# 192 turns (128x128 transposes) move from TensorE to VectorE's 32x32 blocks and a scratch in DRAM

## The chip, the cores and the metric

One core of one Trainium2 chip runs one program. The metric is the device time of that program in microseconds (us), the median of several runs. TensorE is called PE, VectorE DVE, ScalarE ACT, GpSimd POOL and SyncE SP, as the profile does.

## The reference, cut to what matters

```python
# x: (1, 256, 2048) float32; one layer
h = rmsnorm(x, g_mix)
q_r, f_r, i_r, og_r, q_a, k_a, v_a, gate_a, gate_b = split_columns(h @ w_in)
# (A) gated linear recurrence, 16 heads of 128, chunks of 64 positions
f = lb + (1 - lb) * sigmoid(f_r); k = 1 - f; b = cumsum(log f) in a chunk
a = (silu(q_r) * exp(b - b_mid)) @ (k * exp(b_mid - b)).T, causal
o_a = a @ i_r + (q * exp(b)) @ state, normed, * silu(og_r)
# (B) attention over a band of 2 chunks, 32 heads of 64, 4 key heads, rotary, a sink
pr = softmax([q k^T, sink]); o_b = pr @ v
x = x + concat(sigmoid(gate_a) * o_a, sigmoid(gate_b) * o_b) @ w_out
h = rmsnorm(x, g_mlp)
x = x + square(relu(h @ w_up)) @ w_down
x = x + sigmoid(x @ w_ple_gate) * (p @ w_ple_proj)
return rmsnorm(x, g_final)
```

## The kernel before, in words

All weights stream from DRAM once, in 588 chunks of 256 rows x 512 columns (512 KB). A chunk is loaded by SP into one of `RAW_SLOTS` = 4 buffers (`w_raw`). ACT then copies it to a rounded float (`w_hi`, line 977, in `split_hi`) and DVE subtracts to get the rest (`w_lo`, line 1334, in `split_lo`), each into one of `W_SLOTS` = 4 buffers. PE multiplies: per chunk four matmuls of the activations' high part and four of their low part with `w_hi` (lines 678 and 679), then four with `w_lo` (line 684). The buffers come back in order: SP's load of chunk n waits for `w_lo` of chunk n-4, ACT's split of chunk n waits until PE has used chunk n-4.

The work between the products is written into the same order by hand. Each engine has a function `steps(n)`. PE calls it behind chunk n; ACT and DVE run `LAG` = 3 chunks ahead of it, so they call `steps(n)` behind their split of chunk n+3. All waits are in the order of the program on each engine: whoever waits holds up everything behind it there, the splits of later chunks too.

Before the output projection of the mixer there are four head groups (j = 0 to 3), each with blocks of 8 chunks: qa, gb, f, q, then i, og, ga (for j > 0 the 16 chunks of the output projection of the group before, `wo`, stand between q and i). A position in group j is counted from the first chunk of f: `a = n - A0[j]` for the attention, `h = n - H0[j]` for the recurrence; both have the same zero. The tables `SCORES`, `F_TURN`, `Q_TURN`, `DECAY`, `KE_TURN` and others say at which position a step stands.

PE turns what the products leave with positions on partitions into channels on partitions, by a product with an identity matrix (`turn`, line 720, and `weights_turn`, line 759) into a PSUM bank: per group the rotated queries (`zb`, 8 turns), f (`za`, 8), q (`zb`, 8), the attention weights (`pr`, 16) and the merge gate (`sgb`, 8). ACT or DVE takes each from PSUM (for `pr`: DVE's copy to `pT`, line 1490). The turns of `x_sb`, `u_sb`, and `gate` are others, and stay. `weighted_values` is the product of the turned weights with the values (line 771), `scores` the product of line 747, and `recurrence_scores` and `late_scores` (lines 787, 791, 804) use what DVE makes of f and q; PE waits there for `ke_ready` (line 1641).

After the mixer come the 128 `up` chunks, of which the last 112 have the weights as the stationary operand (`turned_chunk`, lines 692 and 698), the `down` chunks, and the gate at the end.

Of the kernel before, what the change touches and what calls it, by code (L numbers as in the profile page):

```python
# [34 lines left out]
P = 128  # L35
TT = 2
# [97 lines left out]
def program(nc, x, p, positions, g_mix, w_in, lb_logits, hgrn_norm_g, sinks, w_out,  # L134
            g_mlp, w_up, w_down, w_ple_gate, w_ple_proj, g_final, out):
    with ExitStack() as ctx:
# [29 lines left out]
        with ExitStack() as mix:  # L166
# [25 lines left out]
            pT = mb("pT", [P, 2, 4, P])  # L192
# [79 lines left out]
        kTd_out = sem("kTd_out")  # L272
        qaT_out = sem("qaT_out")
        nm_ready = sem("nm_ready")
        pr_ready = sem("pr_ready")
        pT_out = sem("pT_out")
# [50 lines left out]
        out_stored = sem("out_stored")  # L327

# [94 lines left out]
        for j in range(NG):  # L423
            for t in range(TT):
                use(("qaT", j, t), t, qaT_out, 2 * j + t + 1)
            for t in range(TT):
                for hh in range(2):
                    use(("score", j, t, hh), hh, pr_ready, 4 * (2 * j + t + 1))
                for g in range(2):
                    use(("pT", j, t, g), g, pT_out, 2 * (2 * j + t) + g + 1)  # L430
            use(("pv", j, 1), 0, pv_out, 2 * j + 2)
            for t in range(TT):
                use(("gbT", j, t), t, am_ready, 2 * j + t + 1)
            for hp in range(2):
                use(("fT", j, hp), 2, f_exp, 2 * j + hp + 1)
                if hp == 0:
                    use(("pv", j, 0), 2, pv_out, 2 * j + 1)
                use(("qT", j, hp), 3, q_ready, 2 * j + hp + 1)
                use(("late", j, hp), 2, late_out, 2 * j + hp + 1)
                use(("aT", j, hp), 3, am_masked, 2 * j + hp + 1)  # L440
# [81 lines left out]
        def parts_of(t):  # L522

            return ((slice(0, CHUNK), CHUNK), (slice(CHUNK, P), P)) if t == 0 else ((slice(0, P), P),)

# [7 lines left out]
        def _(sp):  # L533
# [40 lines left out]

            for slot in HEAD:
                load(slot)
                if slot[0] in (1, 2, 3):
                    load_x(slot[0])
            for r in range(ROUNDS):
                for slot in BODY:  # L580
                    load(slot, r)
# [60 lines left out]
        def _(pe):  # L642
# [9 lines left out]
            def chunk(slot, r=0):  # L652
# [13 lines left out]

                s = n % W_SLOTS
                pe.wait_ge(w_hi_ready, count(n + 1, r, LOOP_CHUNKS))
                if turned(kind, j):
                    turned_chunk(n, col, c, s, first, last, r)  # L670
                    return
# [16 lines left out]
            def turned_chunk(n, col, c, s, first, last, r):  # L688

                for kk in range(2):  # L690
                    for ct in range(4):
                        pe.matmul(turned_acc(col, ct)[:], w_hi[:, s, kk, ct * P:(ct + 1) * P],  # L692
                                  hT[:, 2 * c + kk].rearrange("p a t c -> p (a t c)"),
                                  start=first and kk == 0, stop=False)
                pe.wait_ge(w_lo_ready, count(n + 1, r, LOOP_CHUNKS))
                for kk in range(2):
                    for ct in range(4):
                        mm = pe.matmul(turned_acc(col, ct)[:, 0:TT * P], w_lo[:, s, kk, ct * P:(ct + 1) * P],  # L698
                                       hT_hi[:, 2 * c + kk].rearrange("p t c -> p (t c)"), start=False,
                                       stop=last and kk == 1)  # L700
                mm.then_inc(w_used, 1)
# [24 lines left out]
            def head_turn(kind, j, hp, src):  # L726

                turn((kind, j, hp), lambda i: src[:, i % 2, (2 * hp + i // 2) * P:(2 * hp + i // 2 + 1) * P])

# [22 lines left out]
            def weights_turn(j, t, g):  # L752
                name = ("pT", j, t, g)
                pe.wait_ge(pn_ready, 2 * (2 * j + t) + g + 1)
                signal, value = bank_free(name)
                pe.wait_ge(signal, value)
                for i in range(4):
                    hh, pair = i // 2, 2 * g + i % 2
                    mm = pe.transpose(bank(name)[:, i * P:(i + 1) * P], pr[:, pair, hh, 0:P], ident[:])  # L759
                mm.then_inc(full(name), 1)  # L760

            def weighted_values(j, t):

                name = ("pv", j, t)
                pe.wait_ge(pT_out, 2 * (2 * j + t + 1))
                signal, value = bank_free(name)
                pe.wait_ge(signal, value)
                parts_ = ((0, slice(0, P)),) if t == 0 else ((V_MIXED, slice(0, CHUNK)), (V_LATE, slice(CHUNK, P)))
                for v, qs in parts_:
                    for hh in range(2):  # L770
                        mm = pe.matmul(four(bank(name)[hh * HD:(hh + 1) * HD, :])[:, :, qs], vv[:, v, j, :],  # L771
                                       pT[:, hh, :, qs], start=True, stop=True, skip_group_check=True)
# [58 lines left out]
            def steps(n):  # L831
# [4 lines left out]
                for j in range(NG):  # L836
                    a, h = n - A0[j], n - H0[j]
                    if a == -3:
                        for t in range(TT):
                            pe.wait_ge(qa_rotated, 2 * j + t + 1)  # L840
                            turn(("qaT", j, t), lambda i: zb[:, t, i * P:(i + 1) * P])
                    for t in range(TT):
                        if a == SCORES[t]:
                            scores(j, t)
                            if t == 1:
                                weighted_values(j, 0)
                        for g in range(2):
                            if a == SCORES[t] + 7 + 2 * g:
                                weights_turn(j, t, g)
                    if a == PV1:  # L850
                        weighted_values(j, 1)
                    if a == ATT_END:
                        for t in range(TT):
# [97 lines left out]
        def _(act):  # L951
# [27 lines left out]

            def sum_squares(t, stage, squares):  # L980
# [32 lines left out]
            def exponentials(j, t, pair):  # L1013

                if pair == 0:
# [5 lines left out]
                    if j or t:  # L1021
                        act.wait_ge(pT_out, 2 * (2 * j + t))
# [11 lines left out]
            def steps(n):  # L1034
# [29 lines left out]
                for j in range(NG):  # L1064
# [3 lines left out]
                    if a == -2:  # L1068
                        for t in range(TT):
                            act.wait_ge(full(("qaT", j, t)), nth(("qaT", j, t)))  # L1070
                            act.activation(qT[:, :, t, :], four(bank(("qaT", j, t))[:]), ACT.Copy)\
# [19 lines left out]
                    if a == ATT_END + 1:  # L1091
                        for t in range(TT):
                            act.wait_ge(am_ready, 2 * j + t + 1)
                            act.activation(mT_hi[:, 4:8, t, :], four(sgb[:, t]), ACT.Copy).then_inc(moA_hi, 1)
# [7 lines left out]
                    if h == OG_END[j]:  # L1102

                        if j:
                            act.wait_ge(gated, 2 * j)
                        z_out("og", j, eg, og_exp, ACT.Exp, NR)
                    if h == GA_END[j]:
                        act.wait_ge(qa_rotated, 2 * (j + 1))
                        if j:
                            act.wait_ge(gated, 2 * j)  # L1110
                        z_out("ga", j, eg2, ga_exp, ACT.Exp, NR)
# [13 lines left out]
                    for hp in range(2):  # L1125
                        i = 2 * j + hp
                        if h == F_TURN[hp] + 1:
                            act.wait_ge(full(("fT", j, hp)), nth(("fT", j, hp)))
# [687 lines left out]
```

## Time and profile before

| | |
|---|---|
| median of 3 runs | 1716.59 us (1716.02 to 1717.23) |
| the profiled execution, its own time | 1718.0 us |
| its span, first to last instruction | 1716.3 us |
| PE busy | 1696.1 us, 99% |
| DVE busy | 1102.8 us, 64% |
| ACT busy | 925.0 us, 54% |
| DMA moved | 315.30 MB, mean 184 GB/s |

The table says what share of the span an engine had an instruction under way. Waits are in other views: a row that ends with an arrow names what the engine waited for, and the rows of a timeline give start and duration of each instruction, so that the step from one start to the next is what an instruction costs a busy engine.

### The profile page before, as it was taken

The numbers are of one execution on the slowest core, as the hardware profiler recorded it, in microseconds if no ns is written. First come the engines' busy times: TensorE is split into PE (matmuls) and PEld (weight loads), VectorE is DVE, ScalarE is ACT, GpSimd is POOL, SyncE is SP. The second block draws the span as 40 slices with busy tenths as digits, with TensorE's granted clock in tenths as the row PEclk, the third lists the DMA queues.
The fourth block names the chain that finished last, engine by engine and source line by source line (L and its number), as shares of the span: only waits on it lengthen the run. The fifth ranks groups of instructions, "written<-read, shape, count | busy, mean of one in ns | idle before, by whom it ended". The sixth has DMA issues, their size and how long they took to land.

```text
span 1716.3 us, 22351 instructions
## 1 busy us (share of the span) xinstructions
PE 1696.1 (99%) x8669; PEld 1416.6 (83%) x8669; DVE 1102.8 (64%) x1405; ACT 925.0 (54%) x1227; POOL 16.9 (1%) x72
## 2 busy tenths in 40 slices
PE   7999999999999999999999999999999999999997
PEld 6888888788887888878888888888888888888886
DVE  6667866875668756687585565656555556566565
ACT  6466647655565555655546554544444445454454
POOL 3000000000000000000000000000000000000000
PEclk9999999999999999999999999999999999999999
DMA  6655555556655566555556666666666665655554
GB/s 216 203 174 180 173 173 168 176 176 181 185 180 173 173 183 185 173 173 176 181 177 212 186 192 191 190 190 193 190 193 188 194 189 193 190 190 187 181 184 136
DMA packets 163292, 315.30 MB, mean 184 GB/s; under 512 B 10161, under 2 KB 10482, under 8 KB 163058
## 3 DMA queue, kind: packets, MB, share of 16 engines
q1 hardware_dynamic: 162016, 312.01, 59.5%
q10 hardware_dynamic: 1170, 1.87, 0.3%
q8 instruction: 68, 1.11, 0.3%
q14 instruction: 38, 0.31, 0.1%
HBM read 311.74 MB, written 2.10 MB: 183 GB/s over the span
## 4 chain that ended last, share of the span: by engine, by line
PE 98%; DVE 1%; ACT 1%; DMA 0%; issue 0%; SPq 0%; DVEq 0%; ACTq 0%
PE acc L678 22%; PE acc L679 22%; PE acc L684 22%; PE acc L692 6%; PE turn L692 6%; PE turn L678 3%; PE turn L679 3%; PE turn L684 3%; PE turn L698 3%; PE acc L698 3%; PE turn L720 2%; PE turn L747 0%; PE turn L771 0%; PE turn L820 0%; PE turn L759 0%; DMA w_raw<-in_w_in_dram 0%
## 5 line engine op out<-in xcount | busy, mean ns | idle before, releaser
L1334 DVE TENSOR_TENSOR w_lo<-w_raw,w_hi 128x1024 fp32r<-128x1024 f32 x588 | 720.0, 1224 | 562.9 <-ACT w_hi L977 560.2
L977 ACT ACTIVATE w_hi<-w_raw 128x1024 fp32r<-128x1024 f32 x588 | 622.7, 1059 | 700.7 <-PE acc L684 444.9
L678 PE MATMUL acc<-w_hi,hT 128*128 128x512 f32 x1104 | 435.6, 395 | 4.4 <-ACT w_hi L977 4.4
L679 PE MATMUL acc<-w_hi,hT 128*128 128x512 f32 x1104 | 431.1, 390 | 0.0
L684 PE MATMUL acc<-w_lo,hT 128*128 128x512 f32 x1104 | 296.2, 390 | 0.0
L678 PEld LDWEIGHTS acc<-w_hi,hT 128*128 128x128 f32 x1104 | 207.8, 188 | 48.4 <-ACT w_hi L977 5.6
L684 PEld LDWEIGHTS acc<-w_lo,hT 128*128 128x128 f32 x1104 | 207.8, 188 | 43.6
L679 PEld LDWEIGHTS acc<-w_hi,hT 128*128 128x128 f32 x1104 | 208.0, 188 | 41.9
L678 PE MATMUL acc<-w_hi,mT_hi 128*128 128x512 f32 x416 | 164.4, 395 | 0.0
L679 PE MATMUL acc<-w_hi,mT_lo 128*128 128x512 f32 x416 | 162.2, 390 | 0.0
L692 PE MATMUL acc<-hT,w_hi 128*128 128x512 f32 x448 | 140.0, 394 | 0.0
L692 PE MATMUL turn<-hT,w_hi 128*128 128x512 f32 x448 | 138.7, 390 | 0.0
L684 PE MATMUL acc<-w_lo,mT_hi 128*128 128x512 f32 x416 | 111.3, 389 | 0.0
L692 PEld LDWEIGHTS turn<-hT,w_hi 128*128 128x128 f32 x448 | 84.1, 188 | 19.1
L678 PEld LDWEIGHTS acc<-w_hi,mT_hi 128*128 128x128 f32 x416 | 78.1, 188 | 18.0 <-ACT w_hi L977 2.4
L684 PEld LDWEIGHTS acc<-w_lo,mT_hi 128*128 128x128 f32 x416 | 78.1, 188 | 16.4
L679 PEld LDWEIGHTS acc<-w_hi,mT_lo 128*128 128x128 f32 x416 | 78.2, 188 | 15.5
L698 PE MATMUL turn<-hT,w_lo 128*128 128x256 f32 x448 | 90.3, 283 | 0.0
L698 PE MATMUL acc<-hT,w_lo 128*128 128x256 f32 x448 | 89.5, 282 | 0.0
L692 PEld LDWEIGHTS acc<-hT,w_hi 128*128 128x128 f32 x448 | 77.4, 190 | 10.1
L698 PEld LDWEIGHTS acc<-hT,w_lo 128*128 128x128 f32 x448 | 77.0, 190 | 8.7
L698 PEld LDWEIGHTS turn<-hT,w_lo 128*128 128x128 f32 x448 | 69.5, 191 | 0.0
(247 smaller groups left out, 1545.7 us busy)
## 6 DMA issues: line engine op xcount, KB each, us to landing
w_raw<-in_w_in_dram SPq DMA_DIRECT2D x232, 512.0 KB, 3.7
w_raw<-in_w_up_dram SPq DMA_DIRECT2D x128, 512.0 KB, 3.8
w_raw<-in_w_down_dram SPq DMA_DIRECT2D x128, 512.0 KB, 4.3
w_raw<-in_w_out_dram SPq DMA_DIRECT2D x64, 512.0 KB, 3.8
w_raw<-in_w_ple_gate_dram SPq DMA_DIRECT2D x32, 512.0 KB, 4.6
x_sb<-in_x_dram SPq DMA_DIRECT2D x8, 256.0 KB, 7.4
w_raw<-in_w_ple_proj_dram SPq DMA_DIRECT2D x4, 512.0 KB, 3.7
out_dram<-x_sb SPq DMA_DIRECT2D x6, 256.0 KB, 3.1
```

Of the source, the lines that this page charges most:

```text
L678: pe.matmul(a, hi[:, k, t, :], w_hi[:, s, kk, :], start=first and kk == 0, stop=False)
L679: pe.matmul(a, lo[:, k, t, :], w_hi[:, s, kk, :], start=False, stop=False)
L684: mm = pe.matmul(acc_of(kind, j, col, t)[:], hi[:, k, t, :], w_lo[:, s, kk, :], start=False, stop=last and kk == 1)
L692: pe.matmul(turned_acc(col, ct)[:], w_hi[:, s, kk, ct * P:(ct + 1) * P], hT[:, 2 * c + kk].rearrange("p a t c -> p (a t c)"), start=first ...
L698: mm = pe.matmul(turned_acc(col, ct)[:, 0:TT * P], w_lo[:, s, kk, ct * P:(ct + 1) * P], hT_hi[:, 2 * c + kk].rearrange("p t c -> p (t c)") ...
L720: mm = pe.transpose(bank(name)[:, i * P:(i + 1) * P], src(i), ident[:])
L977: act.activation(w_hi[:, n % W_SLOTS], w_raw[:, n % RAW_SLOTS], ACT.Copy)\
L1334: dve.tensor_tensor(w_lo[:, n % W_SLOTS], w_raw[:, n % RAW_SLOTS], w_hi[:, n % W_SLOTS].bitcast(F32), ALU.subtract).then_inc(w_lo_ready, 1)
```

## The change

Per group six tensors (`TURNED`: the queries "qa", "f", the weights of the first 128 positions "p0", "q", the gate "gb", the weights of the others "p1") no longer go through PE:

1. DVE turns each 32x32 block in its place (`turn_blocks`, two instructions of 128x512 each) into one of two buffers, `eg` and `eg2` in turn (4 KB a partition), which the gates use later in the group.
2. SP stores the buffer to a scratch in DRAM, so that the blocks come to stand where the whole turn puts them: four stores of 128 KB, each from 32 partitions, in rows of 1 KB. Two are issued behind the load of weight chunk a+8, two behind that of a+9, if DVE turned at position a.
3. ACT's queue loads the 512 KB back in one transfer at position a+4 (`load_turned`), over `zb`, `za`, `sgb` or into `pT`. ACT waits there for the four stores.
4. The users read the blocks from SBUF: ACT's exponentials and DVE's products of f, q and the gate, ACT's copy of the queries to `qT`, and PE's `weighted_values`.

The positions move; `weighted_values` of the first half no longer stands right behind `scores` of the second. Apart from this, the 112 `up` chunks with stationary weights go in pairs: both chunks' `w_hi` products, then both chunks' `w_lo` products.

```diff
-            pT = mb("pT", [P, 2, 4, P])
+            pT = mb("pT", [P, 4, 2, 4, 32])
-        SCORES, PV1, ATT_END = (4, 16), 28, 31
-        F_TURN, Q_TURN, DECAY, KE_TURN = (9, 26), (17, 28), (20, 35), (25, 40)
+        SCORES, VALUES, ATT_END = (6, 18), (21, 33), 36
+        F_TURN, Q_TURN, DECAY, KE_TURN = (14, 31), (22, 34), (25, 37), (30, 42)
+        TURN_AT = {"qa": -4, "f": 9, "p0": 12, "q": 17, "gb": 20, "p1": 24}
+        TO_STORE, TO_LOAD = (8, 9), 4
...
+            def store_turned(kind, j, half):
+                i = turn_number(kind, j)
+                sp.wait_ge(blocks_turned, 2 * (i + 1))
+                rows_ = turned_rows[i].rearrange("(c i) b x -> b i c x", c=4)
+                for b in (2 * half, 2 * half + 1):
+                    sp.dma_start(rows_[b], whole(blocks[i % 2])[32 * b:32 * b + 32]).then_inc(blocks_stored[i % 2], 16)
...
+            def turned_pair(n, col, c, last, r):
+                for c_, s in ((c, n % W_SLOTS), (c + 1, (n + 1) % W_SLOTS)):
+                    pe.wait_ge(w_hi_ready, count(n + 1 + c_ - c, r, LOOP_CHUNKS))
...
-                    if a == -3:
-                        for t in range(TT):
-                            pe.wait_ge(qa_rotated, 2 * j + t + 1)
-                            turn(("qaT", j, t), lambda i: zb[:, t, i * P:(i + 1) * P])
...
-                            if t == 1:
-                                weighted_values(j, 0)
-                        for g in range(2):
-                            if a == SCORES[t] + 7 + 2 * g:
-                                weights_turn(j, t, g)
-                    if a == PV1:
-                        weighted_values(j, 1)
-                    if a == ATT_END:
-                        for t in range(TT):
-                            pe.wait_ge(gb_sig, 2 * j + t + 1)
-                            turn(("gbT", j, t), lambda i: sgb[:, t, i * P:(i + 1) * P])
+                        if a == VALUES[t]:
+                            weighted_values(j, t)
...
-                        if h == F_TURN[hp]:
-                            pe.wait_ge(f_out, 2 * (j + 1))
-                            head_turn("fT", j, hp, za)
-                        if h == Q_TURN[hp]:
-                            pe.wait_ge(q_out, 2 * (j + 1))
-                            head_turn("qT", j, hp, zb)
...
+            def load_turned(kind, j):
+                i = turn_number(kind, j)
+                if kind == "p0" and j:
+                    act.wait_ge(full(("pv", j - 1, 1)), nth(("pv", j - 1, 1)))
+                if kind == "p1":
+                    act.wait_ge(full(("pv", j, 0)), nth(("pv", j, 0)))
+                act.wait_ge(blocks_stored[i % 2], 64 * (i // 2 + 1))
...
+                act.dma_start(to, turned_rows[i][:]).then_inc(landed, 16)
...
+            def turn_blocks(kind, j):
+                i = turn_number(kind, j)
+                if i >= 2:
+                    dve.wait_ge(blocks_stored[i % 2], 64 * (i // 2))
...
+                for part in range(2):
+                    if kind in ("p0", "p1"):
+                        dve.transpose(to[:, 4 * part:4 * part + 4], pr[:, :, part, 0:P].rearrange("p k (b c) -> p k b c", b=4))\
+                           .then_inc(blocks_turned, 1)
...
-                            if a == SCORES[t] + 8 + 2 * g:
-                                name = ("pT", j, t, g)
-                                dve.wait_ge(full(name), nth(name))
-                                dve.tensor_copy(pT[:, :, 2 * g:2 * g + 2, :],
-                                                bank(name)[:].rearrange("p (h k c) -> p h k c", h=2, k=2))\
-                                   .then_inc(pT_out, 1)
```

On PE, group 0, at position 16 before: the scores of the second half of the positions (line 747), and right behind them the values' product of the first half (line 771), between the products of two chunks:

```order
L679 MATMUL acc<-w_hi,hT 128x512
L684 MATMUL acc<-w_lo,hT 128x512 x4
L747 MATMUL turn<-kTd,qT 64x128 x16
L771 MATMUL turn<-pT,vv 64x512 x2
L678 MATMUL acc<-w_hi,hT 128x512
```

And now, three chunks behind those scores (lines 718, 719, 724 and 801 are the former 678, 679, 684 and 771):

```order
L724 MATMUL acc<-w_lo,hT 128x512 x4
L801 MATMUL turn<-pT,vv 64x512 x2
L718 MATMUL acc<-w_hi,hT 128x512
L719 MATMUL acc<-w_hi,hT 128x512
L718 MATMUL acc<-w_hi,hT 128x512
```

The values' product stands in a gap of its own, and no turn of `pr`, `za`, `zb` or `sgb` is left between the chunks.

On ACT, group 0, from position 10 on before: the exponential of f out of the PSUM bank that PE turned it into (line 1129), then the logarithm and the exponential one step on, between the splits of the chunks (977), and at position 16 the move of q out of PSUM (1010):

```order
L1129 ACTIVATE hf<-turn 128x512
L977 ACTIVATE w_hi<-w_raw 128x1024
L1132 ACTIVATE hf<-hf 128x512
L1133 ACTIVATE hf<-hf 128x512
L977 ACTIVATE w_hi<-w_raw 128x1024 x2
L1139 ACTIVATE hg<-hf 128x512
L977 ACTIVATE w_hi<-w_raw 128x1024 x3
L1010 ACTIVATE zb<-acc,stat 128x512 x2
```

And from position 12 on now (line 988 is the split, 1002 the load back, 1162 the exponential of f, 1034 the move of q out of PSUM):

```order
L988 ACTIVATE w_hi<-w_raw 128x1024 x2
L1002 DMA za<-turned_rows 128x1024
L988 ACTIVATE w_hi<-w_raw 128x1024 x2
L1162 ACTIVATE hf<-za 128x512
L988 ACTIVATE w_hi<-w_raw 128x1024
L1002 DMA pT<-turned_rows 128x1024
L1034 ACTIVATE zb<-acc,stat 128x512 x2
L1166 ACTIVATE hf<-hf 128x512
L1167 ACTIVATE hf<-hf 128x512
```

Each load with its wait stands ahead of the splits of the chunks behind it; the exponential of f comes two splits after its load.

On DVE, group 0, from position 12 on before (line 1334 is the split, 1490 a copy to `pT`, 1602 the sum of f's logarithms):

```order
L1490 COPY pT<-turn 128x2x256
L1592 TENSOR_SCALAR hf<-hf,one_lb,lb 128x256 x2
L1334 TENSOR_TENSOR w_lo<-w_raw,w_hi 128x1024
L1596 TENSOR_SCALAR hk<-hf 128x512
L1334 TENSOR_TENSOR w_lo<-w_raw,w_hi 128x1024
L1490 COPY pT<-turn 128x2x256
L1602 SCALAR_TENSOR_TENSOR hb<-smask,hg 128x512
L1604 TENSOR_TENSOR hd<-hb 128x512
L1334 TENSOR_TENSOR w_lo<-w_raw,w_hi 128x1024 x3
```

And from position 17 on now (line 1369 is the split, 1497 a turn of blocks):

```order
L1497 STREAM_TRANSPOSE eg<-zb 128x4x4x32 x2
L1642 TENSOR_SCALAR hf<-hf,one_lb,lb 128x256 x2
L1369 TENSOR_TENSOR w_lo<-w_raw,w_hi 128x1024
L1646 TENSOR_SCALAR hk<-hf 128x512
L1369 TENSOR_TENSOR w_lo<-w_raw,w_hi 128x1024
L1463 TENSOR_REDUCE asc<-turn 128x4 x2
L1467 SCALAR_TENSOR_TENSOR asc<-asc,sink_bc 128x8
L1469 TENSOR_SCALAR asc<-asc 128x8
L1652 SCALAR_TENSOR_TENSOR hb<-smask,hg 128x512
L1654 TENSOR_TENSOR hd<-hb 128x512
L1369 TENSOR_TENSOR w_lo<-w_raw,w_hi 128x1024
L1497 STREAM_TRANSPOSE eg<-sgb 128x4x4x32 x2
```

Turns of blocks stand where the copies to `pT` stood, and the second half's maxima (1463) now stand in one step with the sums of the logarithms (1652).

## Rows read from the trace of the kernel before

**Rows 1.** The page: span, busy engines, granted clock, chain that ended last.

```profile
span 1716.3 us, 22351 instructions
...
PE 1696.1 (99%) x8669; PEld 1416.6 (83%) x8669; DVE 1102.8 (64%) x1405; ACT 925.0 (54%) x1227; POOL 16.9 (1%) x72
...
PEclk9999999999999999999999999999999999999999
```

**Rows 2.** Waits: engine, line, waited for whom: us in total, times, longest.

```profile
PE acc L678 <- ACT w_hi L977: 4.4, 1, 4.4
...
ACT w_hi L977 <- PE acc L684: 444.9, 305, 4.2
```

**Rows 3.** Timeline of PE, group 0: start, us, line, operation; turns between chunks.

```profile
113.16 0.60 PE L720 MATMUL turn<-ident,za 128*128 128x128 f32 x4
...
116.36 0.39 PE L678 MATMUL acc<-w_hi,hT 128*128 128x512 f32 x1
...
119.08 0.60 PE L759 MATMUL turn<-ident,pr 128*128 128x128 f32 x4
...
181.87 1.04 PE L720 MATMUL turn<-ident,sgb 128*128 128x128 f32 x8
...
185.49 0.39 PE L678 MATMUL acc<-w_hi,hT 128*128 128x512 f32 x1
```

**Rows 4.** Groups of PE's instructions by line: count, busy us, mean ns.

```profile
L759 PE MATMUL turn<-ident,pr 128*128 128x128 f32 x64 | 9.6, 272 | 0.0
```

**Rows 5.** Timeline of PE: scores alone, then scores with values behind them.

```profile
97.35 1.07 PE L684 MATMUL acc<-w_lo,hT 128*128 128x512 f32 x4
...
99.38 0.50 PE L678 MATMUL acc<-w_hi,hT 128*128 128x512 f32 x1
...
132.71 1.07 PE L684 MATMUL acc<-w_lo,hT 128*128 128x512 f32 x4
...
135.75 0.50 PE L678 MATMUL acc<-w_hi,hT 128*128 128x512 f32 x1
```

**Rows 6.** Timeline of PE in an `up` block with stationary weights.

```profile
953.69 0.63 PE L692 MATMUL acc<-hT,w_hi 128*128 128x512 f32 x2
...
955.53 0.40 PE L698 MATMUL acc<-hT,w_lo 128*128 128x256 f32 x2
...
956.49 0.63 PE L692 MATMUL acc<-hT,w_hi 128*128 128x512 f32 x2
```

**Rows 7.** Groups of instructions by line, DVE.

```profile
L1490 DVE COPY pT<-turn 128x512 f32<-128x512 f32 x16 | 11.0, 689 | 0.4
```

**Rows 8.** Timeline of ACT at rest: one split for each chunk of PE.

```profile
843.20 1.06 ACT L977 ACTIVATE w_hi<-w_raw 128x1024 fp32r<-128x1024 f32 x1 [1.66 <-PE acc L684]
```

**Rows 9.** DMA issues: queue, count, KB each, median us to landing.

```profile
w_raw<-in_w_down_dram SPq DMA_DIRECT2D x128, 512.0 KB, 4.3
...
x_sb<-in_x_dram SPq DMA_DIRECT2D x8, 256.0 KB, 7.4
...
out_dram<-x_sb SPq DMA_DIRECT2D x6, 256.0 KB, 3.1
```

**Rows 10.** The tile `w_raw`: duration of one DMA issue on SP.

```profile
L573 SPq DMA_DIRECT2D w_raw<-in_w_in_dram x232: 367/368/689, 2.6 to 826.6; - x116
```

**Rows 11.** Timeline, group 1: DVE's steps and its split of chunk 105, PE's use.

```profile
317.34 1.29 DVE L1415 TENSOR_TENSOR x_sb<-acc,x_sb 128x512 f32<-128x512 f32 x2
318.54 0.68 DVE L1441 TENSOR_REDUCE asc<-pr 128x4 f32<-128x516 f32 x1
...
320.08 0.69 DVE L1613 TENSOR_TENSOR hq<-turn,hq 128x512 f32<-128x512 f32 x1
...
321.93 0.69 DVE L1618 TENSOR_TENSOR hf<-hb 128x512 f32<-128x512 f32 x1
...
325.00 1.23 DVE L1334 TENSOR_TENSOR w_lo<-w_raw,w_hi 128x1024 fp32r<-128x1024 f32 x1
...
330.11 1.07 PE L684 MATMUL acc<-w_lo,mT_hi 128*128 128x512 f32 x4
```

More of the change, by code:

```diff
@@ L272, in program @@
         kTd_out = sem("kTd_out")
+        blocks_turned = sem("blocks_turned")
+        blocks_stored = [sem(f"blocks_stored{i}") for i in range(2)]
+        qaT_landed = sem("qaT_landed")
         qaT_out = sem("qaT_out")
+        fT_landed = sem("fT_landed")
+        qT_landed = sem("qT_landed")
+        gbT_landed = sem("gbT_landed")
+        pT_landed = sem("pT_landed")
         nm_ready = sem("nm_ready")
         pr_ready = sem("pr_ready")
-        pT_out = sem("pT_out")
         pv_out = sem("pv_out")
@@ L327, in program, with turn_number, turned_block, whole @@
         out_stored = sem("out_stored")
+        TURNED = ("qa", "f", "p0", "q", "gb", "p1")
+        turned_rows = [nc.dram_tensor(f"turned_rows{i}", [P, 4, 256], F32, kind="Internal")
+                       for i in range(NG * len(TURNED))]
+        blocks = (eg, eg2)
+        def turn_number(kind, j):
+            return len(TURNED) * j + TURNED.index(kind)
+        def turned_block(tile, m0, nm):
+            return tile.rearrange("p b (m c) -> p m b c", c=32)[:, m0:m0 + nm]
+        def whole(tile):
+            return tile[:].rearrange("p t (b x) -> p (t b) x", b=2)
         def count(value, r=0, per=0):
@@ L578, in _ @@
                     load_x(slot[0])
+                for j in range(NG):
+                    for kind in TURNED:
+                        for half in range(2):
+                            if slot[0] == A0[j] + TURN_AT[kind] + TO_STORE[half]:
+                                store_turned(kind, j, half)
             for r in range(ROUNDS):
@@ L686, in chunk @@
                 mm.then_inc(w_used, 1)
[L688 to L701, printed above, removed]
+            def turned_pair(n, col, c, last, r):
+                for c_, s in ((c, n % W_SLOTS), (c + 1, (n + 1) % W_SLOTS)):
+                    pe.wait_ge(w_hi_ready, count(n + 1 + c_ - c, r, LOOP_CHUNKS))
+                    for kk in range(2):
+                        for ct in range(4):
+                            pe.matmul(turned_acc(col, ct)[:], w_hi[:, s, kk, ct * P:(ct + 1) * P],
+                                      hT[:, 2 * c_ + kk].rearrange("p a t c -> p (a t c)"),
+                                      start=c_ == 0 and kk == 0, stop=False)
+                for c_, s in ((c, n % W_SLOTS), (c + 1, (n + 1) % W_SLOTS)):
+                    pe.wait_ge(w_lo_ready, count(n + 1 + c_ - c, r, LOOP_CHUNKS))
+                    for kk in range(2):
+                        for ct in range(4):
+                            mm = pe.matmul(turned_acc(col, ct)[:, 0:TT * P], w_lo[:, s, kk, ct * P:(ct + 1) * P],
+                                           hT_hi[:, 2 * c_ + kk].rearrange("p t c -> p (t c)"), start=False,
+                                           stop=last and c_ > c and kk == 1)
+                    mm.then_inc(w_used, 1)
             def stationary_ready(kind, j, r):
@@ L750, in scores, with weighted_values @@
                                 mm.then_inc(full(name), 1)
-            def weights_turn(j, t, g):
-                name = ("pT", j, t, g)
-                pe.wait_ge(pn_ready, 2 * (2 * j + t) + g + 1)
+            def weighted_values(j, t):
+                name = ("pv", j, t)
+                pe.wait_ge(pT_landed, 16 * (2 * j + t + 1))
                 signal, value = bank_free(name)
                 pe.wait_ge(signal, value)
[L757 to L769, printed above, removed]
+                parts_ = ((0, slice(0, 4)),) if t == 0 else ((V_MIXED, slice(0, 2)), (V_LATE, slice(2, 4)))
+                for v, bs in parts_:
                     for hh in range(2):
-                        mm = pe.matmul(four(bank(name)[hh * HD:(hh + 1) * HD, :])[:, :, qs], vv[:, v, j, :],
-                                       pT[:, hh, :, qs], start=True, stop=True, skip_group_check=True)
+                        out_ = bank(name)[hh * HD:(hh + 1) * HD, :].rearrange("p (k b c) -> p k b c", k=4, b=4)
+                        mm = pe.matmul(out_[:, :, bs], vv[:, v, j, :], pT[:, bs, hh].rearrange("p b k c -> p k b c"),
+                                       start=True, stop=True, skip_group_check=True)
                 mm.then_inc(full(name), 1)
@@ L1067, in steps @@
                         z_out("qa", j, za, qa_out)
-                    if a == -2:
+                    for kind in TURNED:
+                        if a == TURN_AT[kind] + TO_LOAD:
+                            load_turned(kind, j)
+                    if a == 3:
+                        act.wait_ge(qaT_landed, 16 * (j + 1))
+                        if j:
+                            for hh in range(2):
+                                act.wait_ge(full(("score", j - 1, 1, hh)), nth(("score", j - 1, 1, hh)))
                         for t in range(TT):
-                            act.wait_ge(full(("qaT", j, t)), nth(("qaT", j, t)))
-                            act.activation(qT[:, :, t, :], four(bank(("qaT", j, t))[:]), ACT.Copy)\
+                            act.activation(qT[:, :, t, :].rearrange("p k (b c) -> p k b c", b=4), by_tile(zb, t), ACT.Copy)\
                                .then_inc(qaT_out, 1)
```

73 lines of the change are left out of this document (44 added, 29 removed).

## The prediction

> **What bounds the kernel now.** I read the page first. PE is busy for 1696.1 of 1716.3 us and its granted clock is in the top tenth in all 40 slices, its full level of 2.4 GHz; DVE and ACT have 64% and 54% [rows 1]. Then the waits: after the start PE waits for nobody. The one long wait on a split is 4.4 us in the first chunk, while ACT spends 444.9 us of its time waiting for PE to free a buffer [rows 2]. So the time is the sum of what PE issues, and an instruction taken from PE is worth its step from start to start, as long as the splits still come early enough. How early do they come? At rest ACT starts a split the moment PE is through with chunk n-4, needs 1.06 us and has 1.66 us over before the next [rows 8]. PE comes to the `w_lo` products of chunk n three chunks of 2.72 us and 1.81 us later. With 1.23 us for DVE that is a lead of 3 x 2.72 + 1.81 - 1.06 - 1.23 = 7.7 us. The tightest place in a head group that I found is chunk 105: `w_lo` ready at 325.00 + 1.23 = 326.23, used at 330.11, a lead of 3.9 us [rows 11].
>
> **PE: the turns.** A turn's own duration is 272 ns [rows 4], but turns overlap. What counts is the period of a chunk. Without turns it is 119.08 - 116.36 = 2.72 us. With four turns ahead of it, it is 116.36 - 113.16 = 3.20, so 0.48 us for four; with eight, 185.49 - 181.87 = 3.62, so 0.90 us [rows 3]. A group loses two gaps of eight (queries, gate) and eight of four (f, q two each, weights four): 2 x 0.90 + 8 x 0.48 = 5.64 us. Two of the fours share their gap with other matmuls, which stay and pay the change of shape themselves; I take 0.08 us off for these together. Four groups: 22.3 us. Bounds: 192 x (0.60 - 0.27) / 3 = 21.1 us (the step between turns in a row of four, and nothing around it) and 22.6.
>
> One rule speaks against taking turns from PE. The Trainium skill, "VectorE: DVE Perf Modes", "Rules for kernel authors", advises TensorE for a 128x128 transpose if its result may lie in PSUM, because VectorE only turns 32x32 blocks. By it the detour through DRAM must cost more than it saves. In this trace PE is the engine without idle time, and DVE has 36% over, so I follow the rows.
>
> **PE: what is added.** `weighted_values` of the first half used to share a gap with the scores. With scores alone, the step from the last `w_lo` products to the next chunk is 99.38 - 97.35 = 2.03 us; with values behind them 135.75 - 132.71 = 3.04, so 1.01 us for the values in company [rows 5]. Alone they must pay a change of shape on both sides, as the scores do; I choose a quarter of the 1.01 on top, 0.24 us, four times: 0.95 us. Bounds: 0 and 4 x 0.5.
>
> **PE: the pairs.** An `up` chunk takes 956.49 - 953.69 = 2.80 us: 1.84 for the eight `w_hi` products, 0.96 for the eight `w_lo` ones [rows 6]. At 2.72/12 = 0.227 each the first eight would take 1.81. The surplus, 0.02 us net of a slightly shorter first `w_lo` step, stands behind the change from `w_lo` to `w_hi`, and a pair makes that change half as often: 112 x 0.02 / 2 = 1.1 us gained. Bounds 0 and 2. In exchange the first chunk of a pair is freed 1.84 us later. The lead there is 7 us or more and falls to 5: free.
>
> PE's sum: -22.3 + 0.95 - 1.1 = -22.4 us if nobody is late.
>
> **DVE.** Added are 48 turns of blocks, 128x512 each; removed are 16 copies of 689 ns [rows 7]. No row shows a turn of blocks. Nearest is that copy, so I take 0.69 us, 1.4 us for each of the 24 pairs. Bounds: 0.35 and 1.4 us per instruction, half and double. The sum, 33 - 11 = 22 us, lies beside 606 us of PE and costs nothing in total. What counts is positions 17 to 26 of groups 1 to 3, where the work is dense: three pairs of turns 4.1 us, two normalisations at 320.08 - 318.54 = 1.54, the step of decays 325.00 - 321.93 = 3.07, two additions of projection blocks at 1.20 (all [rows 11]), and five 128x512 operations at 0.69, a scan taken double, four of half the cost and two tiny ones, 6.8 us as an estimate. That is 19.5 us against 10 x (2.72 - 1.23) = 14.9 us of free time. The lead of 7.7 us loses 4.6 and wins 2.2 from PE's own gaps (scores, values).
>
> **ACT and the round trip.** Six times a group ACT waits for stores. Stores three and four of a tensor turned at a are issued behind weight load a+9, which waits for `w_lo` of chunk a+5. From there: two issues of 0.37 us [rows 10] and the store behind a 512 KB load in the same queue. Loads land in 4.3 us, a 256 KB store of the output in 3.1, the loads of x, crowded at the start, in 7.4 [rows 9]. I take 0.74 + 4.3 = 5.0 us; bounds 3.9 and 8.1. Measured from PE's start of chunk a+5, `w_lo` of a+5 is ready at 1.81 - 7.7 = -5.9 and the stores have landed at -5.9 + 5.0 = -0.9 us. ACT comes there behind its split of a+7, at 2 x 2.72 - (3 x 2.72 - 1.06) = -1.7. It waits 0.8 us, within its free 1.66. When ACT is already late the stores follow later too. The worst is position 16: the wait for the weights, then 2.5 us of q and f. I get ACT 3.4 us late there. It passes this on to DVE, whose lead is then 7.7 - 4.6 + 2.2 - 3.4 = 1.9 us: still no wait for `w_lo`. The reload, at 4.3 us, lands at 3.4; its earliest reader on ACT stands behind the split of a+9, at 3.8.
>
> The next thing to be late is `ke`. DVE makes it behind its split of chunk 31, 1.1 us on, and PE wants it 1.81 us before that chunk's `w_lo`: a lead of 2.9 us is used up. After position 27, where DVE has nothing to do, it is back at about 1.9 + 1.5 - 1 = 2.4 (the 1 us is my estimate for the gaps between some thirty instructions). So PE waits some 0.5 us for `ke_ready`, in groups 1 to 3: 1.5 us. Behind it the `w_lo` splits catch up. If this cover is thinner, each us more of round trip or each 0.3 us more for a turn of blocks costs about 1 us a group.
>
> SP: 96 stores and waits for `blocks_turned`. DVE signals before its split of a+4, and SP reaches the store only behind that split, so this wait is empty; 96 x 0.37 us of issue fit between loads 2.72 us apart. The loads queued behind a store land perhaps 1 us later, which the 4 buffers absorb.
>
> **The sum.** -22.4 + 1.5 = -20.9 us. Against the profiled execution, whose own time is 1718.0 us, that gives 1697.1 (it stands 1.4 us above the median of the runs). On the median: 1716.6 - 20.9 = 1695.7.
>
> **The rivals.**
> 1. *Hardly a wait*: up to 3 us lost in all, 1694.2 to 1697.2. For it: PE's 7.7 us of lead. This is my forecast, 0.62.
> 2. *A new wait in the dense stretch*, for `ke_ready` or `w_lo`, of 1 to 4 us a group. With a round trip of 6 to 7 us instead of 5, or 1 us for a turn of blocks, 4 to 14 us come back: 1698 to 1709. For it: chunk 105's lead of 3.9 us with less work than now. Chance 0.28.
> 3. *Slower than before*: the round trip holds ACT, place `load_turned` of the weights and the gate. To eat 22.4 us it has to cost 5.6 us a group, 5.2 more than now reckoned. At 1 us a group for each us beyond 5, and double that beyond 8, where weight loads behind the stores are late as well, this decides at 8 + (5.2 - 3) / 2 = 9.1 us. At 11 us it is (3 + 6) x 4 = 36 us: 1695.7 + 36 = 1732. Against it: the highest row is 7.4 us. Chance 0.05, and 0.02 for an end within 0.2%.
> 4. *Turns are dearer on PE than the periods show*. 192 x 0.27 us = 52 us would give 1665. The Trainium skill, "TensorE: Matmul & The Clock Gate", "Part 4: PE-mode transpose", gives about 275 ns for one in a kernel's context. The rows have the same 272 ns as a duration but 0.12 us as the price. Chance 0.03, with any other gain above 25 us.
>
> **Numbers.** Predicted 1695.7 us. The low end of the range is everything hidden, values at no extra, pairs worth 2 us: 1716.6 - 22.3 - 2 = 1692.3. The high end is the round trip at its bound of 8.1 us, 3.1 us a group more: 1695.7 + 12.4 = 1708. No change is within 0.2%, 3.4 us, about what runs of this kernel can tell apart. Faster 0.93, same 0.02, slower 0.05.
>
> **What would show it.** PE's waits: none but the start, or short ones at line 804's `ke`. No turns of `za`, `zb`, `pr`, `sgb`; each former gap's chunk at 2.72 us. DVE's turns of blocks near 0.69 us. ACT's waits for the stores about 1 us each, most behind position 16, the stores landing in 4 to 5 us. The `up` chunks at 2.79 us. The prediction is wrong if PE waits in a head group for more than 3 us, if a turn of blocks takes over 1 us, or if stores land beyond 7 us.

## The result and the profile after

The changed kernel takes 1725.5 us (median of 5 runs, 1723.7 to 1729.1), the kernel before 1716.8 us in its runs beside it: a ratio of 1.0049, 95% interval 1.0038 to 1.0061. It is slower, by 0.5%. The forecast of 1695.7 us and its range up to 1708 us were wrong.

The page of the changed kernel: span, busy engines, shares of the chain that ended last, one row of its DMA issues (count, KB each, median us to landing).

```profile
span 1725.1 us, 22112 instructions
...
PE 1683.8 (98%) x8477; PEld 1398.6 (81%) x8477; DVE 1121.9 (65%) x1437; ACT 922.4 (53%) x1227; POOL 15.7 (1%) x72
...
PE 77%; DVE 9%; ACT 6%; DMA 4%; issue 2%; SPq 1%; ACTq 0%; DVEq 0%
...
turned_rows<-eg SPq DMA_DIRECT2D x96, 128.0 KB, 4.3
```

PE is busy for 12.3 us less than in [rows 1], and the span is 8.8 us longer: PE now waits. The chain that ended last, 98% of it PE's before, now has 77% on PE; the rest runs mostly through DVE, ACT and the stores. The same in four stretches, one for each head group (length, busy us of each engine with its instructions, granted clock, DMA share and GB/s):

```profile
60.00:230.00 170.00, 164.82 (x867) 132.83 (x866) 123.14 (x172) 100.03 (x150) 0.00 (x0) 1.00 0.70 212
230.00:400.00 170.00, 163.50 (x866) 131.77 (x865) 124.65 (x185) 97.04 (x145) 0.00 (x0) 0.99 0.67 207
440.00:610.00 170.00, 165.70 (x867) 133.77 (x866) 125.46 (x180) 97.28 (x143) 0.00 (x0) 0.99 0.69 212
655.00:830.00 175.00, 170.56 (x890) 138.01 (x889) 127.59 (x182) 99.32 (x145) 0.00 (x0) 0.99 0.69 211
```

PE is without work for 5.2, 6.5, 4.3 and 4.4 us, 20.4 us in all; in the same four stretches before it never was. Who waits for whom (us in total, times, longest):

```profile
ACT w_hi L988 <- DMA turned_rows<-eg: 26.0, 8, 4.2
ACT zb L1034 <- DMA turned_rows<-eg: 20.9, 4, 5.5
ACT hq L1182 <- DMA turned_rows<-eg: 12.9, 3, 5.1
ACT pr L1049 <- DMA turned_rows<-eg: 10.1, 4, 2.6
PE turn L834 <- DVE ke L1693: 9.5, 8, 2.3
ACT sgb L1034 <- DMA turned_rows<-eg: 8.5, 3, 3.3
PE acc L718 <- ACT w_hi L988: 6.9, 4, 2.4
ACT val L1034 <- DMA turned_rows<-eg: 3.1, 1, 3.1
PE acc L724 <- DVE w_lo L1369: 2.7, 4, 0.8
```

The six rows with `turned_rows<-eg` are one place in the code: `load_turned`, where ACT waits for the four stores. The name on the left is only what ACT did next. They add up to 81.5 us in 23 waits. PE waits for `ke`, for `w_hi` and for `w_lo`, which before it did only at the start [rows 2].

The timeline of PE, group 0 and an `up` block (start, us, line, operation), answers [rows 3, 5, 6]:

```profile
106.03 1.08 PE L724 MATMUL acc<-w_lo,hT 128*128 128x512 f32 x4
108.76 1.07 PE L724 MATMUL acc<-w_lo,hT 128*128 128x512 f32 x4
...
145.42 1.07 PE L724 MATMUL acc<-w_lo,hT 128*128 128x512 f32 x4
146.42 1.08 PE L801 MATMUL turn<-pT,vv 128*64 128x512 f32 x4
147.43 0.50 PE L718 MATMUL acc<-w_hi,hT 128*128 128x512 f32 x1
...
149.38 0.39 PE L724 MATMUL acc<-w_lo,hT 128*128 128x512 f32 x1
...
963.61 0.63 PE L734 MATMUL acc<-hT,w_hi 128*128 128x512 f32 x2
...
969.18 0.63 PE L734 MATMUL acc<-hT,w_hi 128*128 128x512 f32 x2
```

A chunk without a gap takes 108.76 - 106.03 = 2.73 us. The chunk behind the values' product, standing alone, takes 149.38 - 145.42 = 3.96, so the product costs 1.24 us there; 1.25 was forecast. A pair of `up` chunks takes 969.18 - 963.61 = 5.57, 2.79 a chunk. And DVE's turns of blocks, in the groups of instructions by line:

```profile
L1497 DVE STREAM_TRANSPOSE eg<-zb 128x512 f32<-128x512 f32 x16 | 10.4, 691 | 0.3
```

It takes 0.69 us, as the copy of [rows 7] does.

What one wait looks like: the timeline of group 1 from position 15 on. `eg` holds the turned weights of the first half, stored behind the loads of chunks 100 and 101 (SP); ACT's rows end with the idle time ahead of them.

```profile
297.66 1.30 DVE L1493 STREAM_TRANSPOSE eg<-pr 128x512 f32<-128x512 f32 x2
298.38 2.16 ACT L988 ACTIVATE w_hi<-w_raw 128x1024 fp32r<-128x1024 f32 x2 [2.73 <-DMA turned_rows<-eg]
298.88 3.70 DVE L1369 TENSOR_TENSOR w_lo<-w_raw,w_hi 128x1024 fp32r<-128x1024 f32 x3
300.53 1.06 SPq L607 DMA_DIRECT2D turned_rows<-eg  x2
302.14 1.25 SPq L607 DMA_DIRECT2D turned_rows<-eg  x2
303.06 1.05 ACT L988 ACTIVATE w_hi<-w_raw 128x1024 fp32r<-128x1024 f32 x1
309.60 1.26 ACT L1034 ACTIVATE zb<-acc,stat 128x512 f32<-128x512 f32 x2 [5.49 <-DMA turned_rows<-eg]
311.95 2.14 ACT L988 ACTIVATE w_hi<-w_raw 128x1024 fp32r<-128x1024 f32 x2
...
313.67 0.39 PE L718 MATMUL acc<-w_hi,mT_hi 128*128 128x512 f32 x1
```

ACT is through with its split of chunk 99 at 304.1 and does nothing until 309.2. The last two stores were issued from 302.14 to 303.4, since SP issues them behind a load that waited for `w_lo` of chunk 97, and DVE makes the `w_lo` of chunks 96 to 98 only from 298.88 on, in one go. What kept it was its own step: the normalisation of these weights and the turn of their blocks. ACT's split of chunk 96 had been ready since 298.38 - 2.73 = 295.65. In the kernel with early stores (below), where ACT hardly waits, DVE makes the same three splits in one go behind the same step:

```profile
290.30 3.71 DVE L1369 TENSOR_TENSOR w_lo<-w_raw,w_hi 128x1024 fp32r<-128x1024 f32 x3
```

Behind the wait stand q's move out of PSUM, two steps for f, and only then the split of chunk 100, ready at about 313.0; PE takes it up at 313.67, a lead of 0.7 us where at rest it is 3 x 2.72 - 1.06 = 7.1. Ten chunks later nothing is left of it:

```profile
347.30 1.21 PE L724 MATMUL acc<-w_lo,mT_hi 128*128 128x512 f32 x4 [0.73 <-DVE w_lo L1369]
350.81 0.71 PE L834 MATMUL turn<-qe,ke 128*128 128x128 f32 x4 [2.30 <-DVE ke L1693]
...
352.86 0.80 PE L718 MATMUL acc<-w_hi,mT_hi 128*128 128x512 f32 x1
...
355.95 1.07 PE L724 MATMUL acc<-w_lo,mT_hi 128*128 128x512 f32 x4
```

and the granted clock (the number before the DMA share) of the stretches before and during it:

```profile
345.00:351.90 6.90, 3.87 (x39) 2.60 (x39) 6.82 (x14) 2.67 (x4) 0.00 (x0) 1.00 0.80 250
352.00:355.30 3.30, 3.30 (x36) 2.66 (x30) 3.22 (x4) 1.11 (x2) 0.00 (x0) 0.50 0.91 292
```

PE waits 0.7 and 2.3 us, and then the clock stands at half (1.2 GHz) for 3.4 us, of which the window shows 3.3: the eight `w_hi` products take 355.95 - 352.86 = 3.09 us, where 1.81 is normal. The clock falls once in each of groups 1 to 3 (in group 3 behind a wait of 2.4 us for `w_hi`), never in the head groups of the kernel before. At half speed 3.4 us do the work of 1.7, so it costs some 5 us in all, as an estimate.

### The profile page after: what moved, and what is told of

Read it like the earlier page. It is cut to its first block, busy times and chain, and to the rows that moved or that the text cites. A ratio compares the mean times of both kernels' runs of the same rounds, so it can differ in the third digit from the quotient of the medians.

```text
span 1725.1 us, 22112 instructions
## 1 busy us (share of the span) xinstructions
PE 1683.8 (98%) x8477; PEld 1398.6 (81%) x8477; DVE 1121.9 (65%) x1437; ACT 922.4 (53%) x1227; POOL 15.7 (1%) x72
## 4 chain that ended last, share of the span: by engine, by line
PE 77%; DVE 9%; ACT 6%; DMA 4%; issue 2%; SPq 1%; ACTq 0%; DVEq 0%
PE acc L718 16%; PE acc L719 15%; PE acc L724 15%; PE acc L734 6%; PE turn L734 6%; DVE w_lo L1369 4%; PE turn L719 3%; PE turn L718 3%; PE turn L724 3%; PE turn L741 3%; PE acc L741 3%; DMA turned_rows<-eg 3%; ACT w_hi L988 3%; PE turn L763 1%; DMA w_raw<-in_w_in_dram 1%
## 5 line engine op out<-in xcount | busy, mean ns | idle before, releaser
L734 PEld LDWEIGHTS acc<-hT,w_hi 128*128 128x128 f32 x448 | 81.0, 189 | 14.0
L741 PEld LDWEIGHTS acc<-hT,w_lo 128*128 128x128 f32 x448 | 73.4, 191 | 4.4
```

## The experiments

Eight kernels. The kernel before took 1717.4 us beside the first four and 1717.2 us beside the second four (15 runs each).

### Stores earlier

```diff
-        TO_STORE, TO_LOAD = (8, 9), 4
+        TO_STORE, TO_LOAD = (7, 7), 4
```

> The changed kernel, but all four stores of a tensor stand behind weight load a+7 and not behind a+8 and a+9. They are issued as soon as DVE has turned the blocks, one to two chunks (2.7 to 5.4 us) sooner. Theory A, ACT's in-order waits for the stores (82 us in all, up to 5.5 each) make the splits late and so PE: these waits fall below 20 us, PE's idle time in the head groups (21 us) falls below 5, the time to 1694 to 1700. Theory B, DVE's dense stretch is the cause: the time stays at 1718 to 1726. Theory C, stores in SP's queue hold up the weights: no better, or worse, since SP now waits for DVE before the next load: 1722 to 1730.

Measured: 1697.7 us, ratio 0.9884 (0.9871 to 0.9898). One pair of numbers turns the change from a loss to a gain of 1.2%. From its page and its waits:

```profile
turned_rows<-eg SPq DMA_DIRECT2D x96, 128.0 KB, 2.8
```

```profile
ACT hf L1162 <- DMA za<-turned_rows: 5.5, 4, 1.7
...
ACT zb L1034 <- DMA turned_rows<-eg: 3.3, 4, 1.0
...
PE turn L834 <- DVE ke L1693: 1.5, 4, 0.6
```

ACT's waits for the stores fall from 81.5 us to 3.3; PE keeps four waits for `ke`, 1.5 us together. The stores also land faster, in 2.8 us instead of 4.3. That they stood in SP's queue (theory C) did no harm: they still do, and ACT waits 18.3 us for the weights of `w_in`, in the changed kernel 17.8. DVE's work (B) is the same as in the changed kernel, so it alone is not the cause.

### ACT kept, its load moved to GpSimd's queue

```diff
+            for j in range(NG):
+                for kind in TURNED:
+                    load_turned(kind, j)
...
-                    for kind in TURNED:
-                        if a == TURN_AT[kind] + TO_LOAD:
-                            load_turned(kind, j)
```

`load_turned` is the same, with `pool` in place of `act`; GpSimd has nothing else to do in this part of the program.

> The changed kernel, but the six loads back per group, with their waits for the stores, are issued by GpSimd, which has nothing else to do there; ACT waits only where it reads. The stores are where they were. Theory A: ACT has no wait for stores, only what is left in its waits for the data at its readers (f and q, five to ten us a group at worst); 1696 to 1706. Theory B: 1718 to 1726. Theory C: no change either, 1720 to 1727, for the stores still stand between the weight loads.

Measured: 1699.6 us, ratio 0.9896 (0.9882 to 0.9909). The stores stay at (8, 9) and as slow as they were:

```profile
turned_rows<-eg SPq DMA_DIRECT2D x96, 128.0 KB, 4.4
```

```profile
POOL zb L694 <- DMA turned_rows<-eg: 434.3, 8, 125.7
...
ACT hf L1180 <- DMA za<-turned_rows: 11.8, 4, 3.9
```

GpSimd stands in these waits for hundreds of us, most of them before the blocks are even turned, and that costs next to nothing, since nothing is queued behind. The last of the four stores lands as late as in the changed kernel: 6.4 us on the mean, there 6.3 (T_s in the table further down). So with the same travel of the data it was decisive on whose queue the wait stood. What is left on ACT is the wait for f itself, 11.8 us where the changed kernel has 7.6, and one of 2.9 us for the queries; PE waits 1.7 us for `ke`.

### Nothing stored and nothing loaded

`store_turned` and `load_turned` return at once, and the readers take the tensors as they are, unturned; `pT` is zero. So this kernel leaves out the round trip and the waits that hang on it. DVE's turns and all of PE's work stay.

> The changed kernel without its stores and loads: DVE turns the blocks into eg and eg2, but the readers take the tensor that has not been turned, and the weighted values' product takes a pT of zeros. So the work of PE, ACT and DVE is as in the changed kernel and only the round trip is left out. Theory A: all stalls go, the time is 1694 to 1697, the before less 22. Theory B: DVE has as much to do as before this edit, so at least half of the 31 us of stalls stays: 1709 or more.

Measured: 1697.7 us, ratio 0.9886 (0.9871 to 0.9901), span 1695.2 us. The way through DRAM cost the changed kernel 1725.1 - 1695.2 = 29.9 us of span, and with early stores it costs 1 us. What is left of PE's waits without the round trip is 1.5 us for `ke`.

### The pairs alone

The kernel before with `turned_pair` in place of `turned_chunk`, and nothing else.

> The kernel before, with the up chunks of stationary weights in pairs and nothing else. All theories: 1.1 us less, 1715.6, from half as many changes from w_lo to w_hi products; an up chunk of 2.79 us on the mean and not 2.80. A rival, that the later release of the first chunk of a pair makes PE wait: 1717 or more.

Measured: 1716.0 us, ratio 0.9992 (0.9983 to 1.0000), at the edge of what can be told apart. From the first to the last of the 112 chunks the traces show 573.9 us here and in the changed kernel, 575.0 in the kernel before: 1.1 us less, the value forecast.

### The stores' time, in steps

Two more places of the stores, else the changed kernel: `TO_STORE` (8, 8), and (9, 10).

> All four stores of a turn stand behind the load of chunk a+8, none behind a+9, so the last pair can leave one chunk (2.72 us) sooner; everything else is as in the changed kernel (1725.5 us). Theory A (ACT meets the stores in its own order, waits 2.1 to 5.0 us at each of 24 points, some 19 us a group, and PE stalls only once ACT's lead of about 7 us is used up): each wait shrinks by up to 2.7 us, to 0 to 2.3 us; ACT's free 1.66 us a chunk takes that up between two of them, so nearly the whole gain comes back: 1698 to 1702 us. The price as I predicted it (1 us of round trip costs 1 us a group): 2.7 x 4 = 11 us less, 1714 to 1715 us.

> Both pairs of stores stand one load later, behind the loads of chunks a+9 and a+10, so they land 2.72 us later; the load back stays at a+4. Theory A (no lead is left, so PE pays for nearly all that ACT waits): six waits a group of 2.7 us more, 16 us a group, of which ACT makes good perhaps a third between them: 10 to 16 us a group, 1725.5 + 40 to 65 = 1765 to 1790 us, with the granted clock lower in more places since PE is idle more often. The price as I predicted it, 1 to 2 us a group for each us of round trip: 2.7 x 4 = 11 to 22 us more, 1736 to 1747 us.

Measured: 1702.4 us, ratio 0.9915 (0.9901 to 0.9928), and 1772.1 us, ratio 1.0325 (1.0311 to 1.0339). ACT's waits for the stores with (8, 8), the longest row of five, which add up to 28.7 us in 10 waits:

```profile
ACT hq L1182 <- DMA turned_rows<-eg: 11.7, 3, 4.4
```

and with (9, 10), the longest of six rows for the stores, 134.3 us in 22 waits, and PE's for ACT:

```profile
ACT w_hi L988 <- DMA turned_rows<-eg: 40.9, 6, 7.6
PE acc L718 <- ACT w_hi L988: 36.5, 13, 6.9
```

In the table T_s is the time from the end of `w_lo` of chunk a+5 to the last of the four landings, which the prediction put at 5.0 us, from the 24 turns of each trace.

| stores behind loads | T_s, mean | ACT waits for stores | against before | added per added us of wait |
|---|---|---|---|---|
| a+7, a+7 | - | 3.3 us | -19.8 us | |
| a+8, a+8 | 4.1 us | 28.7 us | -14.8 us | 5.0 / 25.4 = 0.20 |
| a+8, a+9 (the change) | 6.3 us | 81.5 us | +8.7 us | 23.5 / 52.8 = 0.44 |
| a+9, a+10 | 8.9 us | 134.3 us | +54.9 us | 46.2 / 52.8 = 0.88 |

For a+7 the stores hang on `w_lo` of a+3, and T_s says nothing. The waits are the sums of the rows, those for loads not among them. The first us of waiting cost a fifth of their length, the last ones most of it. A part of that bend is the clock, as the head groups of the changed kernel (first row) and of (9, 10) show:

```profile
60.00:830.00 770.00, 749.58 (x3883) 607.61 (x3882) 552.01 (x781) 439.09 (x638) 0.00 (x0) 0.99 0.68 207
60.00:830.00 770.00, 721.03 (x3642) 581.26 (x3641) 516.00 (x730) 412.56 (x606) 0.00 (x0) 0.97 0.65 196
```

PE's idle time rises from 20.4 to 49.0 us, by 28.6 of the 46.2, or 0.54 per us of wait; the clock stands at half for 44.4 us instead of 10.2, which is worth up to 17 us more, as an estimate. From a+7 to (8, 8) PE's idle time there rises by 3.5 us, 0.14 per us of wait, and from (8, 8) to the change by 15.3, 0.29. So the bend is there without the clock too: ACT's lead takes the first waits, and once it is gone PE pays. Per us of round trip and per group that is 23.5 / (4 x 2.2) = 2.7 and then 46.2 / (4 x 2.6) = 4.4 us. Of the expectations, theory A's 1698 to 1702 and 1765 to 1790 held, but for 0.4 us; the linear price gave 1714 and 1736 to 1747.

### DVE's turns twice

With the early stores, DVE makes every pair of turns of blocks twice over.

```diff
+                for part in range(2):
...
+                        mm = dve.transpose(to[:, 4 * part:4 * part + 4], pr[:, :, part, 0:P].rearrange("p k (b c) -> p k b c", b=4))
...
+                    mm.then_inc(turned_once, 1)
+                dve.wait_ge(turned_once, 2 * (i + 1))
```

> The version with early stores (1697.7 us), where DVE makes each pair of turns of blocks twice, 48 instructions of 0.69 us more, 33 us, 4.1 us of it in the dense stretch of each group. The price as I predicted it (each 0.3 us more for a turn of blocks costs 1 us a group): 2.3 us a group, 9 us in all, 1706 to 1708 us, as waits for ke. Rival: DVE's lead, now that ACT is on time again, covers it and only the small waits for ke grow: at most 4 us more, 1698 to 1701.5 us. The stores also start up to 1.4 us later, which theory A prices at nothing while ACT has its lead.

Measured: 1714.2 us, ratio 0.9986 (0.9978 to 0.9995). Both expectations fell: it costs 16.5 us, not 9 and not under 4.

```profile
PE turn L835 <- DVE ke L1703: 9.4, 8, 2.3
```

```profile
341.90 0.87 PE L835 MATMUL turn<-qe,ke 128*128 128x128 f32 x4 [2.29 <-DVE ke L1703]
```

It shows that the early version has little left in and behind the dense stretch, the place of rival 2: with some 4 us more for DVE between positions 17 and 26 PE loses 1.4, 6.6, 3.7 and 5.2 us in the four groups (how far the ends of the chunks in the two traces move apart), nearly all of it at positions 27 to 31. The clock adds to it: 0.50 from 342.3 to 345.7, right behind the wait above, and once more from 769.0 to 772.4. But the doubled turns act on a second way too: with (7, 7) SP waits for DVE's turns before it issues the next weight load. ACT waits for the weights of `w_in` 33.8 us in 22 waits, with the turns made once 18.3 us in 11. How much of the 16.5 us goes each way was not tested.

### `ke` one chunk later

```diff
-        F_TURN, Q_TURN, DECAY, KE_TURN = (14, 31), (22, 34), (25, 37), (30, 42)
+        F_TURN, Q_TURN, DECAY, KE_TURN = (14, 31), (22, 34), (25, 37), (31, 43)
```

> The version with early stores (1697.7 us), where PE takes the products with ke one chunk later (positions 31 and 43 in place of 30 and 42). If the 1.5 us in four waits for ke are all that is left over on PE, they go and nothing takes their place: 1696 to 1697 us. If what waits there is a chain that moves along (DVE's step for ke is placed by the same table and moves too), the wait stays as it is: 1697 to 1698.5 us.

Measured: 1695.6 us, ratio 0.9873 (0.9860 to 0.9887), the fastest of all. No wait of PE for `ke` is left, and the chain lies on PE again:

```profile
span 1693.9 us, 22108 instructions
...
PE 98%; DVE 1%; ACT 1%; DMA 0%; issue 0%; SPq 0%; DVEq 0%; ACTq 0%
```

The span is 1716.3 - 1693.9 = 22.4 us shorter than before, the forecast sum of PE's work with nobody late. By the medians beside each other it is 1717.2 - 1695.6 = 21.6 us, since the profiled run of the kernel before took 1718.0 us, 1.4 us above the median that the forecast starts from.

## Why the prediction was wrong

Right, by its own steps:

- **PE's sum** of -22.4 us. The kernel in which nobody is late has 22.4 by the spans and 21.6 by the medians, so the size is right within 1 us, and the equal last digit is luck. The period of a chunk, not the duration of a turn, was the price; rival 4 fell. (By its own figures the term for the turns is (5.64 - 0.08) x 4 = 22.2 us and not 22.3, which changes nothing.)
- **The values alone** at 1.25 us: 1.24. **The pairs**: 1.1 us. **A turn of blocks** at 0.69 us: 0.69.

Right by luck:

- **`ke` as the next thing to be late, 1.5 us.** With early stores PE waits just 1.5 us for `ke`, but not where the sum had it. The forecast was 0.5 us in each of groups 1 to 3 at the first use, position 30, because of the dense stretch. There PE doesn't wait at all; the four waits, 0.3 to 0.6 us, one in each group, are all at the second use, position 42, as this one of group 1:

```profile
372.29 0.71 PE L834 MATMUL turn<-qe,ke 128*128 128x128 f32 x4 [0.31 <-DVE ke L1693]
```

In the changed kernel itself it was 9.5 us, and not the only wait.

Wrong was the paragraph "ACT and the round trip", in three terms:

1. **"From there: two issues of 0.37 us and the store ... 0.74 + 4.3 = 5.0 us."** T_s was 4.9 to 7.8 us, mean 6.3, in the 24 turns. The last issue came 1.2 us behind `w_lo` and not 0.74 (a store takes 0.47 us to issue by the median, and two of them 1.06 and 1.25 us in the rows of SP at 300.53 and 302.14), and landed 5.1 us later. The median of 4.3 over 96 stores was right, but four stores land when the slowest does: 5.0 took a median where a maximum was needed.
2. **"It waits 0.8 us, within its free 1.66."** The wait is T_s less ACT's way from `w_lo` of a+5 to the end of its split of a+7. I reckoned 4.2 us for that way, with ACT and DVE at rest, one split each 2.72 us. It was 2.4 to 4.1, mean 3.2. ACT's lateness did not shorten it: the mean is 3.1 with early stores and 3.4 with the load on GpSimd, where ACT has next to no wait for stores. Rest was the wrong state to reckon from: at these positions both engines have steps between their splits, as DVE's at 297.66. So 6.3 - 3.2 = 3.1 us a wait, 24 times, in place of 0.8. (The 81.5 us also hold the issue of each load.) With (9, 10), where ACT is latest, the way is 3.3 and the wait 8.9 - 3.3 = 5.6: stores and splits move along together. That is the sentence "When ACT is already late the stores follow later too", which I wrote down and then didn't price: a late ACT doesn't shorten its wait by being late.
3. **"Each us more of round trip ... costs about 1 us a group."** There are six such waits in a group. While ACT has a lead they cost little (0.20 of their length), without it most of it (0.88, the clock included). The measured curve is bent: 5.0 us in all for the step from a+7 to (8, 8), then 2.7, then 4.4 us a group for each us. Hence rival 3 did not need its 9.1 us to reach the time of the kernel before, but some 5.5 (a straight line between the rows of the table); its mechanism was the right one ("the round trip holds ACT"), with a price that was about three to four times too low and a chance, 0.05, that followed from the price. Rival 2 had the measured round trip in its condition, 6 to 7 us, and by the same price gave it 4 to 14 us, where some 30 came.

How much each is worth, as an estimate from the table: between T_s 4.1 and 6.3 us the time rises from -14.8 to +8.7 us; a straight line gives -5.2 at 5.0 us, 1711.6 us. So of the 29.8 us between forecast and result some 14 come from term 1, and 16 would have been there with T_s as forecast, from terms 2 and 3. If the curve bends between the two rows as it does beyond them, the first share is a lower bound.

Not in the prediction at all was PE's clock, about 5 of the 29.9 us of span that the round trip cost. Of the rest 18.9 us are PE's idle time in the four stretches (20.4, less the 1.5 that are there without the round trip); some 6 us I can't place, since the ends of matmuls are modelled.

Where it went: 22.4 us were gained on PE and 22.4 + 8.8 = 31.2 given back, 29.9 us by the round trip (1725.1 - 1695.2) and 1.3 (1695.2 - 1693.9) by the waits for `ke` that are there without it. The 29.9 begin in ACT's queue. That is shown by the two experiments that leave the work and the bytes as they are: the stores earlier, or the wait on another queue. Why the stores land in 2.8 us with (7, 7) and in 4.3 with (8, 9) was not settled. They move the same bytes and stand between the same weight loads; what else is under way beside them differs.

One rule of the Trainium skill, "DMA: Bandwidth & Descriptors", "Rules for kernel authors", puts in a line what the first experiment does: issue a DMA early, do other work, and wait for it late. The runs agree, 1725.5 against 1697.7 us for the same bytes with the wait at its old place.

## What to carry to other kernels

Where an engine that feeds the bound waits in its own program order, don't compare one wait with its spare time: count the waits between two places where it recovers, and ask whether what it waits for hangs on its own progress (here load, split, `w_lo`, store, wait); if so, being late does not shorten the wait. Take the latest of several transfers for such a wait, not their median, and put the wait on a queue with nothing behind it or the transfer one step earlier before judging the idea. A reserve that covers a cost at first makes the price of the next us look small: measure at two points beyond it.

## What the runs showed of the hardware

- An idle time of 2.3 or 2.4 us on PE was followed by 3.4 us at a granted clock of 0.50 (1.2 GHz), in the changed kernel three times; with late stores the clock fell in eleven places in the head groups, behind waits of 1.9 to 6.9 us. With (8, 8), where PE's waits in the head groups were at most 1.1 us long, it never fell there. In the version with doubled turns one wait of 2.3 us of three passed without it, and with late stores one of 2.4, so the length of the wait alone doesn't decide.
- A 32x32-block turn of 128x512 float32 takes 0.69 us on DVE, the same as a copy of that size.
- Stores of 128 KB from 32 partitions, two or four in a row beside a steady stream of 512 KB loads, landed in 2.4 (doubled turns) to 4.4 us (load on GpSimd) by the median, and in the changed kernel the last of four 4.9 to 7.8 us behind the end of `w_lo` of a+5. A load of 512 KB from the scratch took 4.7 us (to `zb`) or 5.2 (to `pT`) by the median there.
